# Third layer's mixer: projections of later chunks and part of the output projection issued between the steps of the linear and the dilated attention

## The reference

```python
u = _rmsnorm(h, norm1_w[l])
proj = u @ w_in[l]
gq, gk, gv, gg, glf, glb, aq, ak, av = jnp.split(proj, split_at, axis=-1)
gla_out = _gla_mixer(gq, gk, gv, gg, glf, glb, gla_fwd_gate_w[l], gla_fwd_gate_b[l],
                     gla_bwd_gate_w[l], gla_bwd_gate_b[l], gla_norm_w[l])
att_out = _dilated_mixer(aq, ak, av)
mixed = jnp.concatenate([gla_out, att_out], axis=-1)
h = h + mixed @ w_out[l]
u = _rmsnorm(h, norm2_w[l])
moe = _hier_moe(u.reshape(B * S, D), router_group_w[l], router_group_b[l],
                router_expert_w[l], router_expert_b[l], expert_w_gate[l],
                expert_w_up[l], expert_w_down[l])
```

## Time and profile before

| | us |
|---|---|
| three runs | 1385.06, 1370.96, 1368.24 |
| median | 1370.96 |
| the profiled execution | 1370.9 |
| its span, first to last instruction | 1369.1 |
| TensorE busy in the span | 1240.8 (91%) |
| VectorE, ScalarE busy | 319.1, 204.4 |
| the chain that ended last: TensorE 73%, DMA 18%, VectorE 4% | |

### The profile page before, as it was taken

How to read it: one execution, slowest core, us unless ns; L and a number is a source line. 1 busy time by engine, 2 the same in 40 slices (tenths; PEclk the granted TensorE clock), 3 DMA queues, 4 the chain that set the end, 5 groups by cost and what they waited for, 6 DMA issues and landing times.

```text
span 1369.1 us, 14568 instructions
## 1 busy us (share of the span) xinstructions
PE 1240.8 (91%) x5882; PEld 623.1 (46%) x5882; DVE 319.1 (23%) x891; ACT 204.4 (15%) x468; POOL 0.7 (0%) x5
## 2 busy tenths in 40 slices
PE   6999998999999998999799879898898999889885
PEld 3546546554477746554364454532242232233221
DVE  1324633121300534111502263510010010000002
ACT  2023502110101612010112122100000000000000
POOL 0000000000000000000000000000000000000000
PEclk9997798999999898999999958899999999999998
DMA  9772022999934011999653300269999999999993
GB/s 351 144 295 105 1 70 95 408 415 395 333 128 176 9 62 67 404 418 403 232 176 126 145 1 15 109 270 428 428 425 429 429 429 428 428 427 427 428 427 161
DMA packets 76872, 364.38 MB, mean 266 GB/s; under 512 B 21234, under 2 KB 26644, under 8 KB 52116
## 3 DMA queue, kind: packets, MB, share of 16 engines
q1 hardware_dynamic: 75876, 361.93, 66.3%
q10 hardware_dynamic: 944, 1.73, 0.4%
HBM read 362.60 MB, written 1.05 MB: 266 GB/s over the span
## 4 chain that ended last, share of the span: by engine, by line
PE 73%; DMA 18%; DVE 4%; issue 2%; ACT 2%; SPq 0%; DVEq 0%; ACTq 0%
DMA weights<-in_expert_w_down_dram 17%; PE bank L649 13%; PE bank L926 13%; PE bank L966 8%; PE bank L675 6%; PE bank L664 6%; PE bank L959 5%; PE bank L990 4%; PE bank L898 2%; PE bank L901 2%; PE bank L732 1%; PE bank L866 1%; PE bank L706 1%; DMA weights<-in_ab_w_in_dram 1%; PE bank L692 1%
## 5 line engine op out<-in xcount | busy, mean ns | idle before, releaser
L926 PE MATMUL bank<-weights,projected 128*64 128x256 f32 (+1 forms) x2048 | 344.2, 492 | 18.7 <-DMA weights<-in_expert_w_gate_dram 9.2
L926 PEld LDWEIGHTS bank<-weights,projected 128*64 128x64 f32 (+1 forms) x2048 | 135.1, 124 | 213.3 <-issue 170.0
L649 PE MATMUL bank<-weights,x_transposed 128*128 128x512 f32 (+1 forms) x416 | 178.9, 589 | 9.6 <-DMA weights<-in_ab_w_in_dram 6.3
L966 PE MATMUL bank<-weights,work 128*32 128x512 f32 x512 | 121.4, 629 | 30.3 <-DMA weights<-in_expert_w_down_dram 30.3
L649 PEld LDWEIGHTS bank<-weights,x_transposed 128*128 128x128 f32 x416 | 79.6, 194 | 101.5 <-issue 96.1
L966 PEld LDWEIGHTS bank<-weights,work 128*32 128x32 f32 x512 | 35.4, 115 | 113.8 <-issue 112.5
L675 PE MATMUL bank<-weights,mixed 128*128 128x512 f32 x192 | 83.2, 594 | 1.6 <-DVE mixed L1695 1.1
L664 PE MATMUL bank<-x_transposed,weights 128*128 128x256 f32 (+1 forms) x352 | 76.4, 379 | 0.0
L1881 DVE COPY work<-bank 128x512 f32<-128x512 f32 (+1 forms) x32 | 22.1, 690 | 209.8 <-PE bank L966 140.4
L664 PEld LDWEIGHTS bank<-x_transposed,weights 128*128 128x128 f32 (+1 forms) x352 | 63.8, 182 | 13.0 <-issue 1.3
L959 PE MATMUL bank<-weights,work 128*32 128x512 f32 x512 | 63.3, 626 | 1.6 <-DVE work L1886 1.6
(11 more groups left out here) (282 smaller groups left out, 990.0 us busy)
## 6 DMA issues: line engine op xcount, KB each, us to landing
weights<-in_expert_w_gate_dram SPq DMA_DIRECT2D x32, 2048.0 KB, 15.6
weights<-in_expert_w_up_dram SPq DMA_DIRECT2D x32, 2048.0 KB, 17.3
weights<-in_expert_w_down_dram SPq DMA_DIRECT2D x32, 2048.0 KB, 17.2
weights<-in_moe_w_gate_dram SPq DMA_DIRECT2D x16, 2048.0 KB, 10.7
weights<-in_moe_w_up_dram SPq DMA_DIRECT2D x16, 2048.0 KB, 12.9
weights<-in_moe_w_down_dram SPq DMA_DIRECT2D x16, 2048.0 KB, 9.8
weights<-in_sb_w_in_dram SPq DMA_DIRECT2D x6, 2048.0 KB, 18.3
weights<-in_w_in_dram SPq DMA_DIRECT2D x6, 2048.0 KB, 15.0
```

The costliest lines, as they stand in the source:

```text
L649: i = mm(BANK[4 + 2 * (seq % 2) + t][:, 0:ncols], XT[:, kt, t * P:(t + 1) * P], w[:, kt, :], start=kt == 0, stop=kt == KT - 1)
L926: i = mm(b[n_slots * c:n_slots * (c + 1), e * F:(e + 1) * F], x[:, kt, q * n_slots:(q + 1) * n_slots], w[c][:, col:col + F], start=kt == 0 ...
L966: i = mm(BANK[2 + half][r0 + n_slots * c:r0 + n_slots * (c + 1), :], hT[:, a * step + f, n_slots * c:n_slots * (c + 1)], slot(n + c)[:, co ...
```

## The change

TensorE's, ScalarE's and VectorE's lists of the third mixer are rewritten, and a few buffers with them:

1. The two low-rank gates become one pass: one tile of 32 columns (8 matmuls instead of 16), result in one `LR` of 32 rows plus a row of ones. The gates' weights `gw` get 33 rows, those of the other direction zero; GpSimd clears them at the start, and SyncE's small loads of them wait for that (`gate_w_cleared`). This chunk is now loaded and projected ahead of q/k, and the gates' matmuls stand in the middle of q/k's projection.
2. GG, AQ, AK and AV are projected in halves of one token tile (`project_half`, 8 matmuls, bank 6 or 7), each put between two steps of the linear attention; AV's quarters stand between the transposes ahead of the dilated attention, the last of them inside it (step 1). ScalarE copies each half with `take_half`. The q/k/AQ/AK transposes move behind the outputs and go to banks 4 and 5, the key-value products and second scores to banks 0 to 3.
3. A quarter of the output projection (the first half of `w_out`, its four `kt` that are the linear attention's result) runs inside the dilated attention, one `kt` for both token tiles at steps 3, 4, 6 and 8 (`out_first`). The rest, 24 matmuls, follows the attention.
4. On VectorE the state recurrence stands ahead of the masks; the rotation of AQ stands between the two masks, that of AK behind the second. ScalarE's list follows.

```diff
-        W2_NCOLS = [512, 512, 32, 512, 512, 512, 512]
-        W2_COL0 = [C_GV, 0, C_LF, C_GG, C_AQ, C_AK, C_AV]
+        W2_NCOLS = [512, 32, 512, 512, 512, 512, 512]
+        W2_COL0 = [C_GV, C_LF, 0, C_GG, C_AQ, C_AK, C_AV]
...
+            def project_half(n, t, k0=0, k1=KT):
+
+                w = slot(n).rearrange("p (k c) -> p k c", k=KT)
+                if k0 == 0:
+                    pe.wait_ge(*HALF_FREE[n, t])
+                    chunk_loaded(n)
+                for kt in range(k0, k1):
+                    i = mm(BANK[6 + t][:, :], XT[:, kt, t * P:(t + 1) * P], w[:, kt, :], start=kt == 0, stop=kt == KT - 1)
+                if k1 == KT:
+                    i.then_inc(half_psum if t == 0 else chunk_done, 1)
+
+            def out_part(n, half, t, bank, kts=range(KT)):
...
-            project_T(N_2 + 1, 13, 4)
-            project_T(N_2 + 2, 14, 2, RANK)
...
-            project(N_2 + 3, CH, 15)
+            project_T(N_2 + 1, 13, 1, 2 * RANK)
...
+            project_T(N_2 + 2, 14, 4, between=gate_inputs)
+            project_half(N_2 + 3, 0)
 
             pe.wait_ge(la_ready, 1)
...
-            for n in range(4, 7):
-                project(N_2 + n, CH, 12 + n)
...
+            project_half(N_2 + 3, 1)
+            project_half(N_2 + 4, 0)
...
+            gla_scores(0, 4)
+            project_half(N_2 + 5, 0)
+            pe.wait_ge(state_ready, 1)
+            gla_scores(1, 0)
+            project_half(N_2 + 5, 1)
+
             pe.wait_ge(att_ready, 1)
-            pe.wait_ge(state_ready, 1)
...
+            project_half(N_2 + 6, 0, 0, 4)
+            dil_transposes(0, AQ)
+            project_half(N_2 + 6, 0, 4, 8)
+            dil_transposes(1, AK)
+            project_half(N_2 + 6, 1, 0, 4)
             pe.wait_ge(go_ready, 1)
...
-            pe.wait_ge(goT_ready, 1)
-            attention(DIL_JOBS, len(AB_JOBS), 8, {})
+            pe.wait_ge(qt_act, 11)
+
+            def out_first(kt):
+                pe.wait_ge(goT_ready, 1)
+                pe.wait_ge(proj_copied, 19)
+                for t in range(T):
+                    out_part(N_2 + 7, 0, t, 6 + t, range(kt, kt + 1))
+
+            attention(DIL_JOBS, len(AB_JOBS), 8, {1: lambda: project_half(N_2 + 6, 1, 4, 8), 3: lambda: out_first(0), 4: lambda: out_first(1),
+                                                  6: lambda: out_first(2), 8: lambda: out_first(3)})
             pe.wait_ge(o_copied, 12)
-            project_out(N_2 + 7)
+            for t in range(T):
+                out_part(N_2 + 7, 0, t, 6 + t, range(4, 8))
+            for t in range(T):
+                out_part(N_2 + 7, 1, t, 4 + t)
```

More of the change, by code:

```diff
@@ L639, in keep_clock_up @@
                     mm(BANK[bank][:, :], ident, XT_[:, 0:CH], start=True, stop=True)
+            HALF_FREE = {}
+            for c in range(4):
+                HALF_FREE[N_2 + 3 + c, 0] = (half_copied, c) if c else (proj_copied, 14)
+                HALF_FREE[N_2 + 3 + c, 1] = (proj_copied, 15 + c) if c else (proj_copied, 14)
             def project(n, ncols, seq, between=None, tiles=range(T)):
@@ L654, in project, with project_T @@
                     i.then_inc(chunk_done, 1)
-            def project_T(n, seq, tiles, width=P):
+            def project_T(n, seq, tiles, width=P, between=None):
                 if seq >= 2:
@@ L665, in project_T @@
                                w[:, kt, c * width:(c + 1) * width], XT[:, kt, :], start=kt == 0, stop=kt == KT - 1)
+                    if c == 1 and between:
+                        between()
                 i.then_inc(chunk_done, 1)
+            def project_half(n, t, k0=0, k1=KT):
[8 more added lines that the diff above has]
+            def out_part(n, half, t, bank, kts=range(KT)):
+                chunk_loaded(n + half)
+                w = slot(n + half).rearrange("p (k c) -> p k c", k=KT)
+                for kt in kts:
+                    i = mm(BANK[bank][:, :], mixT[:, kt, t * P:(t + 1) * P], w[:, kt, :], start=kt == 0, stop=kt == KT - 1)
+                if kts[-1] == KT - 1 and t == T - 1:
+                    i.then_inc(chunk_done, 1)
+                elif kts[-1] == KT - 1 and half:
+                    i.then_inc(out_psum, 1)
             def project_out(n):
                 for half in range(2):
-                    chunk_loaded(n + half)
-                    w = slot(n + half).rearrange("p (k c) -> p k c", k=KT)
                     for t in range(T):
-                        for kt in range(KT):
-                            i = mm(BANK[4 + 2 * half + t][:, :], mixT[:, kt, t * P:(t + 1) * P], w[:, kt, :],
-                                   start=kt == 0, stop=kt == KT - 1)
-                        if half and t == 0:
-                            i.then_inc(out_psum, 1)
-                    i.then_inc(chunk_done, 1)
+                        out_part(n, half, t, 4 + 2 * half + t)
             def attention(jobs, first, pairs0, extras):
@@ L1178, in _ @@
                 i.then_inc(ket_psum, 1)
[L1180 to L1189 removed]
+            project_half(N_2 + 4, 1)
             pe.wait_ge(ket_ready, 2)
@@ L1446, in _, with take_gla_half @@
             ac(W1, W1, ACT.Ln, bias=1.0).then_inc(gz_log, 1)
-            take(15, N_2 + 3, [(t, GG[:, t, :], P, CH, 1.0) for t in range(T)])
+            take(14, N_2 + 2, [(0, gqT, P, CH, SCALE), (1, gkT, P, CH, 1.0)])
+            def take_gla_half(c, t):
+                dst, scale = ((GG, 1.0), (AQ, -SCALE), (AK, 1.0), (AV, 1.0))[c - 3]
+                take_half(N_2 + c, t, dst[:, t, :], scale, c - 2)
+            take_gla_half(3, 0)
             act.wait_ge(bs_ready, 1)
@@ L1479, in _, with dil_heads @@
                 i.then_inc(go_square, 1)
+            def dil_heads(m):
+                for k in range(2):
+                    act.wait_ge(qt_psum, 9 + 2 * m + k + 1)
+                    ac(qk[:, 4 * m + 2 * k:4 * m + 2 * k + 2, :], BANK[4 + k][:, :].rearrange("p (n s) -> p n s", n=2), ACT.Copy).then_inc(qt_act, 1)
+            dil_heads(0)
             act.wait_ge(var_ready, 2 * 5 + 1)
```

133 lines of the change are left out of this document (74 added, 59 removed).

## The result

| | before | changed |
|---|---|---|
| median of the runs, us | 1378.01 (1368.24 to 1393.81, four runs) | 1346.44 (1343.2 to 1350.67, four runs) |
| the profiled execution, us | 1370.9 | 1346.59 |
| its span, us | 1369.1 | 1344.7 |

The ratio is 0.9757, 95% interval 0.9716 to 0.9799: faster by 2.4%, some 33 us (the two medians differ by 31.6). The ratios given here are not those of the medians, and the one in experiment 6 leaves out the slowest of its four runs, 1.6% above the fastest. The forecast was 1338 with a range of 1331 to 1352 and 0.74 for "faster by over 2%".

The account below looks back on a forecast made before the run. The end was taken as the MoE's first used slot plus a constant, set by TensorE's mixer. Work 138.3 plus waits 2.5 gave 140.8 us against 173.4, 32.6 shorter: 1370.9 - 32.6, say 1338 us, range 1331 to 1352.

Parts of the forecast that it names:

- faster by over 2%: Outcome of the whole kernel: a time under 1343.5 us, given a chance of 0.74.
- What bounds the end: Third MoE's DMA-bound weight stream: the end is its first used slot's time plus a constant, so mixer savings arrive one for one.
- The sum at 2.4 GHz: TensorE's work in the third mixer, GV's end to output projection's end, added up at full clock: 138.3 us.
- the ratio 0.54: Narrow work's time at high against low clock, from the first layer's attention; it put the outputs at 7.7 us, from 14.2.
- The dilated attention: Third mixer: 2.2 us a job at 2.4 GHz, 17.6 for eight, plus 10.3 us of fillers; TensorE slower than VectorE.
- The waits: TensorE's remaining idle time in the third mixer: 2.5 us charged for all, with state and decays covered by projection halves.
- What all six gaps were before, 12.2: Upper bound for the remaining waits: TensorE's idle gaps in the third mixer before the change, 12.2 us in all.
- the norm's margin: VectorE's norm ahead of the linear result's transposes, the tightest wait: 4.9 us for copy and rotation, half of it spare.
- the rival of an oscillating clock: Third mixer: TensorE falls to 1.2 GHz at six wide-narrow changes, 1.9 us each, 11.4 in all: 1349 us; 13 in 100.
- 21.5 of the 32.6 us hang on the clock: Third mixer's saving that needs 2.4 GHz: 6.5 us in the outputs and 15 in the dilated attention.
- wide work ended each low stretch: Argument against the rival that the low clock stays through outputs and attention, 45 us: 1383 us; 3 in 100.
- kept it once it had it: Argument for a high clock in the third mixer: the first layer's attention held 2.4 GHz after reaching it.

Follow-up runs that it names:

- experiment 6: The change plus three wide matmuls that compute nothing in each router: median 1342.88 us, ratio 0.9674; with three in the first layer's attention too, one execution 1343.53 us.
- experiment 4: The change plus 16 wide matmuls that compute nothing ahead of the output projection's last part: GV's end to output projection's end 152.3 us, span 1371.9 us.
- experiment 2: The change without output projection pieces inside the dilated attention, their matmuls following behind it: GV's end to output projection's end 146.15 us, against 138.6.
- experiment 3: The change with all of AV's projection moved ahead of the outputs: GV's end to output projection's end 147.9 us, 9.4 more than in the change.
- experiment 5: The change plus three wide matmuls that compute nothing at steps 4 and 5 of the first layer's attention: one execution 1356.86 us.
- experiment 1: The kernel before plus wide matmuls that compute nothing ahead of the state and norm waits: mixer stretch 166.3 us against 173.4, one execution 1374.84 us.
- experiment 7: The change plus three matmuls that compute nothing in each router and nine in the first layer's attention: median 1320.37 us, ratio 0.954.

## Why the prediction was right, and where it was off

- **What bounds the end.** Right. From the seventh slot's issue to the end 468.9 us against 468.2, and experiment 4 moved both together by 13.7 us.
- **The sum at 2.4 GHz.** 138.3 us of work forecast, 136.9 found (138.6 less gaps of 0.34, 0.78 and 0.53 us); the 2.5 us charged for waits were 1.65. Low-rank gates, q/k and gates: 19.6 for 19.5. Outputs 7.9 for 7.7: the ratio 0.54 of the earlier trace rows carried over. Output projection 20.9 for 20.8.
- **The dilated attention** was the term most off: 17.6 + 10.3 = 27.9 us of work forecast, 25.9 found (27.5 less the three gaps). In the change's rows from 803.99 us on, a job's scores take 1.06 us from start to start and its transposes 0.58, and the values of two jobs 1.08: 2.15 a job where 2.2 was laid out. But the scores of the first four jobs, which stand two jobs side by side, take 1.07 us for both (8 records at 792.46) where the sum counted them one by one. The rows had it: 8 records in 2.08 us beside 4 in 2.07. That TensorE is the slower engine in this attention once it has its fillers was right: it stands for 1.65 of 27.5 us. What the prediction did not see is that the fillers also kept the clock: experiment 2 took 6.9 us out and the attention became 0.7 us longer.
- **The waits.** "What all six gaps were before, 12.2" was a misreading: there were nine, 14.4 us, and the three missing ones lay in the attention. The rest was right: state and decays covered; the norm's margin 2.9 us, where 4.9 us less copy and rotation were laid out. The cover's price was given as "what stood there before"; experiment 3 measured it for the norm, 9.4 us with the clock's part.
- **The clock.** Right that it would stay up: 1.00 in all stretches of the mixer, no fall at any of the ten changes between wide and narrow groups, so the rival of an oscillating clock failed. Of "21.5 of the 32.6 us hang on the clock", the outputs' 6.5 were 6.3; the attention's 15 were 10.5, because it was not low to the end of the attention before, and because of the pairs of scores. Two reasons given were wrong. That "wide work ended each low stretch": the long one of before ended at about 833 us in narrow work, and so did that of the first attention at 151 us. That the first layer's attention "kept it once it had it": the same attention had lost it at about 116 us. So the outcome was right, but what holds or raises the clock was not understood; experiment 5 relied on the same idea and missed. The Trainium skill, TensorE: Matmul & The Clock Gate, section "A second HAM failure mode: psum-queue depth-cycling", tells of a clock that swings where TensorE idles briefly between groups of matmuls that cycle through PSUM banks. The mixer of the change, with gaps of 0.34 to 0.78 us, does not show it.
- **The time itself.** 1346.4 for 1338: inside the range of 1331 to 1352, outside the 1333 to 1343 that the forecast gave to itself. The step that was off is not in the mixer: there 34.9 us were saved for 32.6 forecast. It is the base. The sum was set against the profiled execution of before, 1370.9, because that was also the median of three runs. The profiles close the account: the change's came to GV's end 9.4 us later (702.28 against 692.90; 11.1 at the first output projection) with the same work in both, the mixer gave 2.3 us more than forecast, and router and MoE took 1.1 more, which makes 8.2 of the 8.3 us. The base was a low draw: of eleven runs of before in the two comparisons that have several, only one lies below 1370.96. The median of the four in this comparison is 1378, and 1378 less 32.6 is 1345. The spread of the three runs, 17 us, and the earlier trace rows, taken on both sides of the clock's return in one attention, had hinted at it; the prediction used the rows for their ratio only.
- **Luck.** The prediction took "faster by over 2%" to mean under 1343.5 us, counted from 1370.96. The change did not get there (one of four runs did); it counts as over 2% because the base came out higher too.

## What to carry to other kernels

Where one engine waits for a chain on others, cut its next independent block into pieces of the length of the gaps and deal them out; the piece can count twice on TensorE, as work done in the gap and as what keeps its clock (experiments 2 and 3; experiment 5 shows that a few wide matmuls need not keep it). When the last stage is a stream bound by DMA that starts late, what counts is when its first buffer is used, and savings ahead of it arrive in full. Compare stretches that start and end at the same instruction, and look for chance in the others before subtracting from a single execution.

## What the runs showed that was not expected

- Narrow work at the low clock stayed there for very different times: some 48 us in the third mixer before, 20 in experiment 1 and 10 in experiment 2, and in the first attention 34, 48, 58, 61, 68 and 72 us in different executions. All of these stretches ended in narrow work. Where wide matmuls stood in a low stretch of an attention (experiments 3 and 7), it ended while or soon after they ran, and in experiment 7 it had begun without a gap. What decides is open.
- The first attention alone moves the whole by up to 15 us from execution to execution (175 to 190 us at its end), and the 6 us gap ahead of the second layer by some 8 more. 18 matmuls that compute nothing, some 16 us of TensorE's time, made the kernel 26 us faster by the medians, most of it in the first attention.
